# Input tiles of the 256-token products laid 1024 bytes apart, 192 bytes modulo 256 from the weight buffers

## The reference, cut to what matters

```python
h = concat([meta, x])                              # 272 tokens
h = h + hgrn2_mix(h, ...)      # rms_norm(h) @ w_in (2048 x 8192), ... @ w_out
k, v, F = fox_shared_kv(h, ...)                    # rms_norm(h) @ w_kv
h = h + fox_mix(h, ...)        # rms_norm(h) @ w_in (2048 x 4096), attention, ... @ w_out
x = h[:, 16:]                                      # 256 tokens from here on
proj = rmsnorm(x, norm1_w) @ w_in                  # 2048 x 11280
...                                                # conv, long conv, mLSTM, branches
x = x + merged @ w_out
gu = rmsnorm(x, norm2_w) @ w_gate_up               # 2048 x 11264
x = x + (silu(gate) * up) @ w_down                 # 5632 x 2048
return rmsnorm(x, norm_f_w)
```

## Time and profile before

| | |
|---|---|
| device time, median of 3 runs | 2782.64 us (2781.58 to 2782.84) |
| span of the profiled execution | 2782.1 us |
| TensorE busy | 2709.1 us (97%), 21390 matmuls |
| VectorE busy | 1564.9 us (56%) |
| ScalarE busy | 1199.1 us (43%) |
| DMA | 445.95 MB, mean 160 GB/s |

### The profile page before, as it was taken

The page is one execution under the profiler, slowest core; times in us unless marked ns, Lnnn a source line. Parts: engine busy times, 40 slices in busy tenths (PEclk is TensorE's granted clock), DMA queues, the critical chain, the costliest instruction groups (busy, mean ns, idle before and its releaser), DMA issues.

```text
span 2782.1 us, 53198 instructions
## 1 busy us (share of the span) xinstructions
PE 2709.1 (97%) x21390; PEld 2616.9 (94%) x21390; DVE 1564.9 (56%) x1889; ACT 1199.1 (43%) x1395; POOL 34.0 (1%) x47
## 2 busy tenths in 40 slices
PE   8999999999999989999999989899999999999998
PEld 8999999999999989999999974589999999999998
DVE  6445767565465665766644445556565555554443
ACT  5334466443366654533444441124444444443332
POOL 0000011000000000000000000000000000000000
PEclk9999999999999999999999999999999999999999
DMA  6555422555544325555555541035555655555553
GB/s 215 182 173 174 144 99 83 168 176 176 174 160 153 121 92 182 207 187 181 177 185 181 184 147 38 1 106 189 184 181 181 193 181 193 187 186 185 175 189 122
DMA packets 123699, 445.95 MB, mean 160 GB/s; under 512 B 13594, under 2 KB 15925, under 8 KB 123440
## 3 DMA queue, kind: packets, MB, share of 16 engines
q1 hardware_dynamic: 122208, 438.82, 47.8%
q0 software_dynamic: 1360, 5.27, 0.6%
HBM read 441.94 MB, written 2.10 MB: 160 GB/s over the span
## 4 chain that ended last, share of the span: by engine, by line
PE 48%; DVE 2%; ACT 0%; issue 0%; DMA 0%; DVEq 0%; ACTq 0%
PE PS L1678 14%; PE PS L1680 14%; PE PS L1679 14%; PE PS L2073 2%; PE PS L2132 1%; PE PS L2062 1%; PE PS L2084 1%; PE PS L2055 0%; PE PS L1766 0%; DMA y_win<-windows 0%; DVE y_T L1573 0%; DVE y_T L1569 0%; DVE y_T L1566 0%; DVE y_T L1570 0%; PE PS L2146 0%
## 5 line engine op out<-in xcount | busy, mean ns | idle before, releaser
L1678 PE MATMUL PS<-XH,hi 128*128 128x256 f32 (+1 forms) x5152 | 1460.2, 283 | 17.8 <-DVE lo L936 15.2
L1679 PE MATMUL PS<-XL,hi 128*128 128x256 f32 (+1 forms) x5152 | 1456.7, 283 | 0.0
L1680 PE MATMUL PS<-XH,lo 128*128 128x256 f32 (+1 forms) x5152 | 1456.4, 283 | 0.0
L936 DVE TENSOR_TENSOR lo<-raw,hi 128x1024 fp32r<-128x1024 f32 x724 | 877.2, 1224 | 837.7 <-ACT hi L468 826.1
L468 ACT ACTIVATE hi<-raw 128x1024 fp32r<-128x1024 f32 x724 | 759.0, 1058 | 985.5 <-PE PS L1680 958.8
L1678 PEld LDWEIGHTS PS<-XH,hi 128*128 128x128 f32 x5152 | 971.8, 189 | 19.7 <-issue 13.7
L1679 PEld LDWEIGHTS PS<-XL,hi 128*128 128x128 f32 x5152 | 971.6, 189 | 0.2
L1680 PEld LDWEIGHTS PS<-XH,lo 128*128 128x128 f32 x5152 | 971.2, 189 | 0.0
L1740 PE MATMUL PS<-XH,hi 128*128 128x256 f32 (+1 forms) x768 | 231.1, 301 | 0.1
L1742 PE MATMUL PS<-XH,lo 128*128 128x256 f32 (+1 forms) x768 | 217.9, 284 | 0.0
L1741 PE MATMUL PS<-XL,hi 128*128 128x256 f32 (+1 forms) x768 | 217.5, 283 | 0.0
(11 more groups left out here) (323 smaller groups left out, 1604.1 us busy)
## 6 DMA issues: line engine op xcount, KB each, us to landing
raw<-stream SPq DMA_DIRECT2D x828, 512.0 KB, 4.0
H<-h_in SPq DMA_DIRECT2D x4, 544.0 KB, 7.5
y_win<-windows POOLq DMA_DIRECT2D x2, 1024.0 KB, 5.5
out<-H SPq DMA_DIRECT2D x4, 512.0 KB, 3.5
dftm<-dft POOLq DMA_DIRECT2D x1, 1024.0 KB, 6.0
w<-w POOLq DMA_DIRECT2D x2, 512.0 KB, 6.9
ml_m<-mask_ml POOLq DMA_DIRECT2D x1, 512.0 KB, 3.8
a_m<-masks_a POOLq DMA_DIRECT2D x1, 272.0 KB, 5.6
```

The source lines that it names most:

```text
L936: dve.tensor_tensor(lo[s][:, :], raw[s][:, :], hi[s][:, :].bitcast(F32), ALU.subtract)\
L1678: pe.matmul(PS[:, bank, 0:n], w_hi, x_hi, start=start, stop=False)
L1679: pe.matmul(PS[:, bank, 0:n], w_hi, x_lo, start=False, stop=False)
L1680: return pe.matmul(PS[:, bank, 0:n], w_lo, x_hi, start=False, stop=stop)
```

## The change

The two buffers become flat, of the same size and at the same place. A view function gives them back as tiles of 272 tokens, as before, or as tiles of 256 tokens that begin `NARROW` = 48 float32 (192 bytes) into the row and follow each other without a gap, 1024 bytes apart. Everything that writes or reads the split activations takes the view of its own token count. In the last stage a buffer of 192 bytes stands in front of `GH`, so that `GH`, `GL`, `g_s` and `g_p` all lie 192 bytes further. The arithmetic, the order of the instructions and the semaphores stay.

```diff
-        XH = sb(ctx, "XH", [P, NT, T], F32R)
-        XL = sb(ctx, "XL", [P, NT, T], F32R)
+        x_hi_flat = sb(ctx, "XH", [P, NT * T], F32R)
+        x_lo_flat = sb(ctx, "XL", [P, NT * T], F32R)
+        NARROW = 48
...
             with ExitStack() as sub:
                 g_scratch = sb(sub, "g_scratch", [P, NT, SEQ])
+            sb(ph, "g_align", [P, NARROW])
             GH = sb(ph, "GH", [P, FT, SEQ], F32R)
             GL = sb(ph, "GL", [P, FT, SEQ], F32R)
...
+        def x_view(flat, n):
+            if n == T:
+                return flat[:, :].rearrange("p (k t) -> p k t", t=T)
+            return flat[:, NARROW:NARROW + NT * SEQ].rearrange("p (k t) -> p k t", t=SEQ)
+        def XH(n):
+            return x_view(x_hi_flat, n)
+        def XL(n):
+            return x_view(x_lo_flat, n)
...
-                    act.activation(XH[:, 4 * q:4 * q + 4, 0:n], scratch[:, 4 * q:4 * q + 4, 0:n], ACT.Copy)\
+                    act.activation(XH(n)[:, 4 * q:4 * q + 4, :], scratch[:, 4 * q:4 * q + 4, 0:n], ACT.Copy)\
...
-                dve.tensor_tensor(XL[:, 4 * k:4 * k + 4, 0:n], src, XH[:, 4 * k:4 * k + 4, 0:n].bitcast(F32),
+                dve.tensor_tensor(XL(n)[:, 4 * k:4 * k + 4, :], src, XH(n)[:, 4 * k:4 * k + 4, :].bitcast(F32),
...
-            def product(q, xh=XH, xl=XL, between={}, pieces=None):
+            def product(q, xh=None, xl=None, between={}, pieces=None):
+                if xh is None:
+                    xh, xl = XH(q.tokens), XL(q.tokens)
...
-                    x_hi, x_lo = XH[:, k, 0:q.tokens], XL[:, k, 0:q.tokens]
+                    x_hi, x_lo = XH(q.tokens)[:, k, :], XL(q.tokens)[:, k, :]
```

More of the change, by code:

```diff
@@ L531, in do @@
                     act.wait_ge(S("xg_ready"), 4 * k + 4)
-                    act.activation(XH[:, 4 * k:4 * k + 4, :], AB[:, 4 * k:4 * k + 4, :], ACT.Copy).then_inc(S("xh_ready"), 1)
+                    act.activation(XH(T)[:, 4 * k:4 * k + 4, :], AB[:, 4 * k:4 * k + 4, :], ACT.Copy).then_inc(S("xh_ready"), 1)
                 return do
@@ L604, in a_split @@
                 act.wait_ge(S("a_gated"), g + 1)
-                act.activation(XH[:, 4 * g:4 * g + 4, :], AQ[:, 4 * g:4 * g + 4, :], ACT.Copy)\
+                act.activation(XH(T)[:, 4 * g:4 * g + 4, :], AQ[:, 4 * g:4 * g + 4, :], ACT.Copy)\
                     .then_inc(S("xh_ready"), 1)
@@ L736, in b_split @@
                 act.wait_ge(S("b_y"), 4 * g + 4)
-                act.activation(XH[:, 4 * g:4 * g + 4, 0:SEQ], BZ[:, 4 * g:4 * g + 4, :], ACT.Copy)\
+                act.activation(XH(SEQ)[:, 4 * g:4 * g + 4, :], BZ[:, 4 * g:4 * g + 4, :], ACT.Copy)\
                     .then_inc(S("xh_ready"), 1)
@@ L867, in mixers @@
                         act.wait_ge(S("y_out"), 4)
-                    act.activation(XH[:, 4 * k:4 * k + 4, 0:SEQ], src, ACT.Copy).then_inc(S("xh_ready"), 1)
+                    act.activation(XH(SEQ)[:, 4 * k:4 * k + 4, :], src, ACT.Copy).then_inc(S("xh_ready"), 1)
             follow(act, prod["br_b"], chunk, mixers, [(2, nothing)], at=3, early={2: tail_w2})
@@ L874, in mixed_piece @@
                 act.wait_ge(chunk_used, prod["br_a" if k < 2 else "out2"].c0 + RING)
-                act.activation(XH[:, 4 * k:4 * k + 4, 0:SEQ], MG[:, 4 * k:4 * k + 4, :], ACT.Copy)\
+                act.activation(XH(SEQ)[:, 4 * k:4 * k + 4, :], MG[:, 4 * k:4 * k + 4, :], ACT.Copy)\
                     .then_inc(S("xh_ready"), 1)
@@ L1719, in mini @@
                         col = slice(128 * kk, 128 * kk + 128)
-                        ins = passes(0, m.tokens, hi[s][:, col], lo[s][:, col], XH[:, k, 0:m.tokens],
-                                     XL[:, k, 0:m.tokens], k == 0, k == NT - 1)
+                        ins = passes(0, m.tokens, hi[s][:, col], lo[s][:, col], XH(m.tokens)[:, k, :],
+                                     XL(m.tokens)[:, k, :], k == 0, k == NT - 1)
                     ins.then_inc(chunk_used, 1)
```

## The result

The changed kernel took 2754.65 us (median of 4 executions) beside 2782.74 us for the kernel before: ratio 0.990, 95% interval 0.9879 to 0.9922. It is faster, as forecast, but by 28 us and not by 64, and outside the range of 2710 to 2731. What was not forecast at all is the spread: its four executions took 2738.13, 2746.03, 2763.27 and 2767.45 us, where those of the kernel before lie within 2.1 us. The profiled execution took 2763.27 us, with a span of 2761.5.

The account below looks back on a forecast made before the run. TensorE's start-to-start matmul step was taken to bound the kernel. `XH`/`XL` products -46.4, `down` -14.2, `b_in` -4.5 and new waits +1.5 summed to -63.6 us: 2782.6 to 2719 us, range 2710 to 2731.

Parts of the forecast that it names:

- What bounds the kernel, and the steps before: Large products: time is matmul count times start-to-start step, 117.7 ns in `gate_up`, 117.8 in the branches, 120.0 in `down`.
- The price of the offset 192: 256-token products: 113.3 ns a matmul at offset 192, against 117.6 for mixed offsets and 120.0 at offset 0.
- A: Rival, 256-token products: the rhythm settles anew at every tile, 115.2 ns a matmul, 2744 us; chance 7%.
- B: Rival: the even 1024-byte step, not the offset, costs `down` its 120.0 ns; about 2811 us, slower; chance 4%.
- C: Rival: no effect, the short tile recurs every four tiles through something other than an address; 2782.6 us; chance 4%.
- The argument against A: `down` changes tiles too and holds 120.0 ns over five tile changes.
- The waits: `w2`: TensorE's four waits for `lo` of a group's fourth chunk grow from 1.0 to 1.3 us each; total charge +1.5 us.
- The stops at the fourth chunk: `w2`, five groups with a convolution but no `SILU`: some 0.3 us slack against 0.31, together 0.3 us as upper estimate.
- The sum: Whole kernel: -46.4 - 14.2 - 4.5 + 1.5 = -63.6 us, giving 2719 us.

Follow-up runs that it names:

- pauses: Changed kernel with TensorE waiting for its own last chunk in each group of the 256-token products, 90 waits: 2782.97 us, ratio 1.0008; with other offsets 2807.58 to 2816.36 us.
- the third profile of the same kernel: Changed kernel unaltered, profiled again beside five timed rounds: 2763.44 us profiled, ratio 0.9844.
- four old tiles: Changed kernel with tiles 0 to 3 of the 256-token view where they were before, tiles 4 to 15 at 192: 2732.97 us, ratio 0.9824.
- one tile at 128: Changed kernel with only tile 0 of the 256-token view at offset 128, tiles 1 to 15 at 192: 2725.18 us, ratio 0.9795.
- `down` alone: Kernel before with the 192 bytes in front of `GH` alone, `XH` and `XL` as before: 2767.12 us, ratio 0.995.

## Why the prediction was wrong

**What bounds the kernel, and the steps before.** Right. The stretches of the earlier trace rows followed TensorE's step in every run.

**The price of the offset 192.** This is the step that failed: "two offsets are priced by the trace itself: 0 costs 120.0, 192 costs 113.3". The first price is good: with pauses 0 keeps 120.0. The second is one of two, and 117.8 is the other. Every stretch at 192 in the trace before came behind a tile at 128, so all its readings had one and the same history, and I read a speed of that history as a property of the address. In the profiled execution 117.8 held in nearly all of `gate_up`, in `down`, in `b_out` and in three fifths of `w2`. By terms, in the 20.6 us by which its span is shorter: `b_in` -5.0 (forecast -4.5), branches and `out2` -6.6 (-6.6), `b_out` 0 (-3.3), `w2` -4.0 (-18.2 and +1.5 of waits), `gate_up` -0.1 (-18.2), `down` -4.7 (-14.2); the rest, -0.2, lies between them. That the branches and `out2` came out to the tenth was the luck of that execution: in the third profile of the same kernel they took nearly what they had taken before the change.

**The rivals.** A (a tile settles anew) is wrong: where the rhythm is fast it holds over all tiles. B (the step of 1024 bytes costs 120.0) is wrong: `down` has kept that step and runs at 113.3 behind the earlier trace rows's layout. C is wrong: the step moved with the offset. The section "Who interferes with whom" of the Trainium skill's page "SBUF — State Buffer" had stood beside C, for TensorE's two independent read ports; what I drew from it, that an address could not matter, is not borne out (116.7 ns at 32, 120.0 at 0). Whether one port waits for the other no run shows. The rival that came true was missing from the list. The argument against A, that `down` holds 120.0 over tile changes, was taken from an offset with one rhythm and said nothing of 192.

**The waits.** The mechanism was right: 4.1 us of waits became 5.0, forecast 5.3. The stops at the fourth chunk of the five groups with a convolution and no `SILU` came too, at 0.04 to 0.24 us each; together they are about 0.8 us, where I had priced 0.3 as an upper estimate. Their larger cost is elsewhere: behind the one at 1248.38 the slow rhythm lasted for 45 us.

**The sum.** The changed kernel's gain is itself no fixed number: 28 us in the first four executions, and 45 in the last five (2738.19 beside 2783.33). None of its ten executions, profiled or not, lies in the range that was given, 2710 to 2731 (worked out, it was 2709 to 2730); the lowest is 2733.86. The direction came out right, for the price of one rhythm that only some stretches had. With the history put right, the same sum holds, in forecasts written before these runs: four old tiles were forecast at 2731 and measured at 2732.97, one tile at 128 at 2724 and 2725.18, `down` alone at 2768.5 and 2767.12.

**What stays open.** Which rhythm an interruption sets. The pauses turned it over in `gate_up` and `down` and not in `w2`. In `gate_up` the profiler's presence seems to go with a different outcome, and three profiles beside seven other executions are few to say so. Nothing here shows why an offset has the step that it has.

## What to carry to other kernels

A price read from a steady stretch is a price for that stretch's history as well; before it is carried over to a stream that runs on unbroken, look for the same operands behind another start. Where a pipelined stream can settle at more than one step, a layout that passes through a setting sequence once a group can be worth more than one that is ideal at every tile. Here twelve matmuls in 192 that cost 5.7 ns more each, and twelve behind them that cost 2.1, kept the other 168 from costing 4.5 more, and the spread was 3 us in four executions where it had been 34 in ten. And when the executions of a deterministic program scatter by 1% while those of its predecessor do not, that is itself a finding, to be looked into before the median is believed.

## What the runs showed of the hardware

- The step of a stream of matmuls, each with its own weight load, moved with the start of the moving operand, counted from the weights modulo 256 bytes: 120.0 ns (0), 116.7 (32), 113.3 or 117.8 (64), 120.0 (96), 118.6 (128), 117.4 or 118.7 (160), 119.3 (176), 113.3 or 117.8 (192), 119.2 (208), 118.3 (224), 117.1 (240), for 256 columns of float32r at the full granted clock. The weights were not moved.
- At 64, 160 and 192 two steps occur. At 192 an uninterrupted stream kept its own over more than 6000 matmuls, through changes of tile, chunk, group, bank and product, and did so at 117.8 ns as well as at 113.3.
- A stop of 0.05 us was enough to pass from one to the other. Longer ones, of 0.2 to 0.4 us, did so in some places and not in others.
- A tile at 128 followed by one at 192 brought the stream to 113.3 ns in every group in which nothing interrupted it, from either speed.
